# PEER's v sums of each layer's first pair of blocks as a dense product with a streamed table, and gathers in stages of u and of v

## The reference

```python
sv, si = lax.top_k(s, PEER_TOPK)                       # s: (tokens, 8, 2, 128)
cand = sv[:, :, 0, :, None] + sv[:, :, 1, None, :]
cv, ci = lax.top_k(cand.reshape(Tb, PEER_HEADS, PEER_TOPK * PEER_TOPK), PEER_TOPK)
...
eidx = i1 * N_KEYS + i2
g = jax.nn.softmax(cv, axis=-1)
u = u_tab[eidx]
v = v_tab[eidx]
a = jax.nn.gelu(jnp.einsum('thkd,td->thk', u, xb).astype(jnp.float32), approximate=False)
return jnp.einsum('thk,thkd->td', (g * a).astype(v.dtype), v)
```

## Time and profile before

| | |
|---|---|
| median of three runs | 3412.68 us (3407.83 to 3419.08) |
| the profiled execution | 3410.22 us, span 3408.4 us |
| TensorE busy | 2653.3 us (78%) |
| VectorE busy | 2352.5 us (69%) |
| GpSimd busy | 2260.1 us (66%) |
| ScalarE busy | 769.2 us (23%) |
| moved | 1187.53 MB, mean 348 GB/s |
| gathers | 1,024 of u and 1,024 of v |

### The profile page before, as it was taken

How to read it: one execution, slowest core, us unless ns; L and a number is a source line. 1 busy time by engine, 2 the same in 40 slices (tenths; PEclk the granted TensorE clock), 3 DMA queues, 4 the chain that set the end, 5 groups by cost and what they waited for, 6 DMA issues and landing times.

```text
span 3408.4 us, 30404 instructions
## 1 busy us (share of the span) xinstructions
PE 2653.3 (78%) x9120; PEld 1550.1 (45%) x9120; DVE 2352.5 (69%) x5335; ACT 769.2 (23%) x1848; POOL 2260.1 (66%) x2059
## 2 busy tenths in 40 slices
PE   8888079898987689778987679988987666556657
PEld 7677057556543256446543246656543222112212
DVE  2327975877689576877699666877689755666564
ACT  2531023442211123332111122442211111111111
POOL 0000276777777776777777776777677777777776
PEclk9879589989999999878999999989999989998899
DMA  5112399999999999999999999999999999999999
GB/s 184 59 50 92 115 385 412 366 322 392 410 362 358 388 410 412 390 331 381 410 381 379 358 383 411 378 322 367 410 394 355 364 401 409 409 409 408 410 409 349
DMA packets 311313, 1187.53 MB, mean 348 GB/s; under 512 B 34544, under 2 KB 34544, under 8 KB 298352
## 3 DMA queue, kind: packets, MB, share of 16 engines
q0 software_dynamic: 294912, 1073.87, 81.8%
q1 hardware_dynamic: 16240, 111.72, 8.4%
HBM read 1183.36 MB, written 2.10 MB: 348 GB/s over the span
## 4 chain that ended last, share of the span: by engine, by line
POOL 30%; PE 26%; DMA 22%; issue 10%; DVE 4%; ACT 1%; ACTq 0%; DVEq 0%; POOLq 0%
DMA v_rows<-expert_v,idx 22%; POOL u_rows L1455 16%; POOL v_rows L1468 15%; PE acc L741 14%; PE bank L457 4%; PE bank L448 4%; DVE arena L1030 1%; PE bank L620 1%; PE bank L439 1%; DVE arena L1288 0%; PE bank L540 0%; DVE arena L1280 0%; DVE arena L1292 0%; DVE X L1410 0%; DVE arena L1318 0%
## 5 line engine op out<-in xcount | busy, mean ns | idle before, releaser
L741 PE MATMUL acc<-v_rows,diag 128*128 128x512 f32 x2988 | 1533.6, 647 | 647.4 <-DMA v_rows<-expert_v,idx 575.6
L1393 DVE CUSTOM_DVE_ANT_0 u_rows<-u_rows,h 128x1024 f32<-128x1024 f32 x1024 | 1247.9, 1224 | 650.5 <-DMA u_rows<-expert_u,idx 646.1
L1455 POOL DMA_INDIRECT u_rows<-expert_u,idx x1024 | 1122.4, 1096 | 685.4 <-DVE idx L1357 348.9
L1468 POOL DMA_INDIRECT v_rows<-expert_v,idx x1024 | 1133.9, 1107 | 404.3 <-issue 249.3
L741 PEld LDWEIGHTS acc<-v_rows,diag 128*128 128x128 f32 x2988 | 560.1, 203 | 1453.1 <-issue 1177.3
L1021 ACT ACTIVATE diag<-consts,wgt 128x128 f32<-128x128 f32 x747 | 286.2, 397 | 1097.8 <-PE acc L741 882.2
L448 PE MATMUL bank<-HT,w_ring 128*128 128x256 f32 x1792 | 405.1, 381 | 2.1 <-DVE HT L1030 2.1
L1410 DVE SCALAR_TENSOR_TENSOR X<-v_rows,wgt,X 128x1024 f32<-128x1024 f32 x277 | 355.7, 1284 | 56.4 <-DMA v_rows<-expert_v,idx 50.7
L448 PEld LDWEIGHTS bank<-HT,w_ring 128*128 128x128 f32 x1792 | 341.3, 191 | 81.3 <-issue 38.7
L457 PE MATMUL bank<-w_ring,HT 128*128 128x256 f32 (+1 forms) x1280 | 274.7, 372 | 0.0
L457 PEld LDWEIGHTS bank<-w_ring,HT 128*128 128x128 f32 x1280 | 236.7, 191 | 50.0 <-issue 21.4
(11 more groups left out here) (185 smaller groups left out, 1860.1 us busy)
## 6 DMA issues: line engine op xcount, KB each, us to landing
w_ring<-weights SPq DMA_DIRECT2D x100, 1024.0 KB, 8.0
u_rows<-expert_u,idx POOLq DMA_INDIRECT x1024, 7.9
v_rows<-expert_v,idx POOLq DMA_INDIRECT x1024, 7.9
X<-in_x SPq DMA_DIRECT2D x2, 1024.0 KB, 6.5
out<-X SPq DMA_DIRECT2D x4, 512.0 KB, 6.5
n2w_wide<-parameters SPq DMA_DIRECT2D x2, 512.0 KB, 8.0
params<-parameters SPq DMA_DIRECT2D x2, 412.0 KB, 7.8
consts<-constants SPq DMA_DIRECT2D x1, 749.5 KB, 6.3
```

The lines of the kernel that those rows point to most:

```text
L741: last = T.matmul(acc[:, at_h], diag[:, i % DIAG_RING], v_rows[:, t % V_RING, at_h], start=(at_t == 0), stop=(t == max(q for q in range(t ...
L1393: made(V.tensor_tensor_reduce(out=rows_u, in0=rows_u, in1=h2[:], scale=1.0, scalar=0.0, op0=ALU.mult, op1=ALU.add, accum_out=dots[:, b % 2 ...
L1455: pool.indirect_dma_start(out=u_rows[:, s % U_RING, :], out_offset=None, in_=u_dram, in_offset=bass.IndirectOffsetOnAxis(ap=idx[:, (n - 1) ...
L1468: pool.indirect_dma_start(out=v_rows[:, t % V_RING, :], out_offset=None, in_=v_dram, in_offset=bass.IndirectOffsetOnAxis(ap=idx[:, t // PE ...
```

## The change

The gathers are now in stages of 256: the two blocks of one pair for u, or for v.

```diff
-PAIRS = BLOCKS // 2
-STEPS = DEPTH * PAIRS
-U_RING, V_RING, DIAG_RING = 6, 6, 5
-LAG = TOPK + 4
-TRUNK_AT, ROUTE_AT, DONE_AT = LAG + 2, 146, PER_STEP - 3
+GROUPS = [(0, 0, 2), (0, 2, 2), (1, 0, 2), (1, 2, 2)]
+STAGE = 2 * SLOTS
+STAGES = [("u", 0, 1), ("u", 1, None), ("v", 1, 2), ("u", 2, 3), ("u", 3, None), ("v", 3, None)]
+GATHERS = STAGE * len(STAGES)
+FOUR, GROUPS_OF_FOUR = 4, P // 4
+ROWS, DIAG_RING = 12, 5
+BESIDE_HOTS, BESIDE_STREAM, STREAM = 10, 6, 3
+EARLY = 40
+ALONE = 18
+def beside(n):
+    at = [e for e, (_, _, m) in enumerate(STAGES) if m == n][0]
+    lo, hi = STAGE * at + (2 if STAGES[at][0] == "u" else 8), STAGE * (at + 1) - 16
+    return lo, lo + (hi - lo) * 58 // 100, hi
+def of_vector(e, r):
+    n = STAGES[e][2]
+    if r < ALONE:
+        return True
+    if n is None:
+        return r % 4 == 3
+    return r % 8 != 0 if STAGE * e + r < beside(n)[1] else r % 3 == 0
```

```diff
+                        hot = hots[i % 2][:, 0]
+                        for t in range(FOUR):
+                            at_t = FOUR * i + t
+                            ins = S.activation(hot[:, t], iota, ACT.Abs, scale=-1.0, bias=first_keyT[:, at_t:at_t + 1])
+                        chain(ins)
+                        made(S.activation(hot, hot, ACT.Relu, scale=-1.0, bias=1.0), "hot1")
...
+                        bank = wait_full(act, f"d{d}.s{b}.{i - 1}")
+                        four = slice(FOUR * (i - 1), FOUR * i)
+                        freed(S.activation(gates[b][:, :, four].rearrange("p i t -> p t i"), bank[:].rearrange("p (t i) -> p t i", t=FOUR), ACT.Copy),
+                              f"d{d}.s{b}.{i - 1}")
...
+                        ins = V.tensor_scalar(hots[i % 2][:, 1, t], iota, second_keyT[b][:, at_t:at_t + 1], weightT[:, at_t:at_t + 1],
+                                              ALU.is_equal, ALU.mult)
...
+                        last = T.matmul(out[:, blk[t]], hots[i % 2][:, 0, t], hots[i % 2][:, 1, t], start=True, stop=True)
```

`gates` of both blocks take 128 KB of each partition, the place of the trunk's tiles (`arena`), the weight ring and `X` of the first pair, which is written to `out` and read back. Then SyncE streams the layer's v table, 64 transfers of two keys (1 MB), and TensorE adds up:

```diff
+                    sy.dma_start(rows[:, at_r:at_r + 2], table[d, :, 2 * j * D:2 * (j + 1) * D].rearrange("i (j d) -> i j d", j=2)
+                                 ).then_inc(sig(f"stream{j % STREAM}"), 16)
...
+                pe.wait_ge(sig(f"stream{j % STREAM}"), 16 * stream_use(d, j))
+                for i in range(2):
+                    key, row = 2 * j + i, rows[:, BESIDE_STREAM + 2 * (j % STREAM) + i]
+                    for b in (1, 0):
+                        for half in range(2):
+                            last = T.matmul(sums[b][half][:, 0:512], gates[b][:, key], row[:, 512 * half:512 * half + 512],
+                                            start=(key == 0), stop=(key == KEYS - 1))
...
+                made(last, "down")
```

Where this stands among the gathers is a second table of slots. Block 0's gates are made beside the end of the first u stage, block 1's at the start of the second, and the product fills the rest of it:

```diff
+    for b, lo, hi in ((0, first + 162, first + STAGE - 4), (1, first + STAGE + 2, first + STAGE + EARLY + 3)):
...
+    lo, hi = first + STAGE + EARLY + 4, first + 2 * STAGE + 4
+    out += [(f"d{j}", lo + (hi - lo) * j / (KEYS // 2)) for j in range(KEYS // 2)]
+    return out + [("xa", hi + 1)]
```

u and v rows now share one ring of 12 row slots. While gates are made u has ten of them, the one-hots two; beside the stream u has six and the stream six. A v gather into a slot that the stream used waits for it:

```diff
+                if kind == "v" and row >= BESIDE_STREAM and (had is None or had // STAGE < e):
+                    wait_down(pool, m // 2, KEYS // 2 - STREAM + (row - BESIDE_STREAM) // 2 + 1)
```

More of the change, by code:

```diff
@@ L181, in phases @@
     tail += [("g0", 0, .4), ("g1", 0, 0), ("g2", 0, 1.2)]
-    return head + middle + cmp_ + att + tail
-PHASES = phases()
-ORDER = {name: i for i, (name, *_) in enumerate(PHASES)}
-assert len(ORDER) == len(PHASES)
-def slots():
-    work = np.array([max(cost) + .5 for _, *cost in PHASES])
-    at, out = ORDER["r0"], []
-    for part, lo, hi in ((work[:at], TRUNK_AT, ROUTE_AT), (work[at:], ROUTE_AT, DONE_AT)):
+    every = head + middle + cmp_ + att + tail
+    if nb == 2:
+        return every
@@ new lines, in phases, with slots @@
+    of_block = ("n1t", "n1e", "xt", "xe", "xp", "dl", "cb", "de", "dm", "yp", "ya", "ys", "nt", "ne", "nc", "nd", "ng", "mt", "me", "n2t", "n2e")
+    return [(x, pe / 2, dve / 2) for x, pe, dve in every if not (x[:3] in of_block and x[3:4] == "1" or x[:2] in of_block and x[2:3] == "1")]
+PHASES = [phases(nb) for _, _, nb in GROUPS]
+ORDER = [{name: i for i, (name, *_) in enumerate(p)} for p in PHASES]
+assert all(len(o) == len(p) for o, p in zip(ORDER, PHASES))
+def slots(n):
+    work = np.array([max(cost) + .5 for _, *cost in PHASES[n]])
+    lo, route, hi = beside(n)
+    at, out = ORDER[n]["r0"], []
+    for part, lo, hi in ((work[:at], lo, route), (work[at:], route, hi)):
@@ L603, in keys @@
                     full(last, f"{n}.nt{b}")
[L604 to L605 removed]
+                out = take(pe, f"{n}.kc", f"ne{nb - 1}")
+                for b in range(nb):
                     last = T.transpose(out[:, blk[b]], nA[:, b, 0:128], ident)
@@ new lines, in tensor_program @@
+        def tensor_program(pe):
+            trunk_run(0, tensor_tracks(pe, 0)).all()
+            run = spread = None
+            for s in range(GATHERS):
+                n, d = starts(s)
+                if n is not None:
+                    run = trunk_run(n, tensor_tracks(pe, n))
+                if d is not None:
+                    spread = dense_run(d, [tensor_dense(pe, d)])
+                if KIND[s] == "v" and not BY_VECTOR[NTH_OF_KIND[s]]:
+                    t, b, at_t = v_slot(s)
+                    by_tensor = [q for q in range(SLOTS) if not BY_VECTOR[t - at_t + q]]
@@ new lines, in pool_program @@
+            trunk_run(0, pool_tracks(pool, 0, chain)).all()
+            run = None
+            for s in range(GATHERS):
+                n, _ = starts(s)
+                if n is not None:
+                    run = trunk_run(n, pool_tracks(pool, n, chain))
+                e, r = divmod(s, STAGE)
+                kind, m, beside_n = STAGES[e]
+                if r == 0 and kind == "u":
+                    pool.wait_ge(sig("idx"), m + 1)
+                row, use, had = ROW_OF[s]
+                if had is not None:
+                    wait_rows_used(pool, had)
+                if kind == "v" and row >= BESIDE_STREAM and (had is None or had // STAGE < e):
+                    wait_down(pool, m // 2, KEYS // 2 - STREAM + (row - BESIDE_STREAM) // 2 + 1)
+                pool.indirect_dma_start(
+                    out=rows[:, row, :], out_offset=None, in_=u_dram if kind == "u" else v_dram,
+                    in_offset=bass.IndirectOffsetOnAxis(ap=idx[:, m % 2, r:r + 1], axis=0),
+                ).then_inc(sig(f"row_in{row}"), 16)
+                if beside_n is not None:
+                    run.after(s - POOL_LAG)
+                    if r == STAGE - 1:
+                        run.all()
```

977 lines of the change are left out of this document (577 added, 400 removed).

## The result

The changed kernel takes 3571.04 us (median of four runs, 3564.33 to 3580.46), beside 3412.86 (3407.83 to 3419.08) for the kernel before on the same chip: 1.0465 times as long, with a 95% interval of 1.0435 to 1.0495. The forecast was 3,480 (2% slower), its range 3,345 to 3,620. The profiled execution took 3580.46 us, at a span of 3578.7.

A forecast was written before the change was run, and what follows sets the result against it. Transfers were taken to bound the kernel before; afterwards each stage has another engine as its bound. 397 + 578 + 543 + 500 + 570 + 543 + 345 + 4 = 3,480 us, 2% slower, range 3,345 to 3,620.

The forecast's parts named there:

- Stages 0: The first trunk alone, the same work as before: 397 us until `idx` is written.
- B: u gathers of a second pair beside the first pair's dense product: 543 us, twice; ScalarE bound first, then TensorE.
- C2: The last stage, v gathers of the second pair with no trunk beside it: 345 us (335 to 365).
- A1: First stage with u gathers of a first pair beside the second's trunk: 578 us, VectorE becoming the bound.
- A2: The same stage as A1 the second time, with no landing to wait for: 570 us.
- its 285: Part before routing in A1 and A2: VectorE 225 us, TensorE 218, and 60 of waits (15 to 110).
- 0.2 us for a one-hot of VectorE: In the routing part of A1 and A2, 32 groups of 4 one-hot instructions: 26 us (20 to 35).
- C1: v gathers of the second pair with a trunk beside them: 500 us, of which 281 before routing and 185 routing.
- Rival 1: Waits of the three trunk stages vanish, VectorE's dots filling the trunk's holes: up to 180 us less, 3,300; chance 0.27.
- Rival 2: ScalarE's strided write of the gates out of PSUM makes a group take 3.6 us: 3,575 us; chance 0.12.
- Rival 3: The stream transfers' wide pitch holds the queues twice as long, 175 us more in each B: 3,830; chance 0.04.

The follow-up runs named there:

- before_thin: The kernel before, with TensorE's v sums cut to 64 of 512 columns, all but a block's first and last: 3411.05 us.
- act_hot2: The changed kernel with block 0's second-key one-hots, weighted, made by ScalarE in place of VectorE: 3518.87 us, 1.0323 times the kernel before.
- split74: The changed kernel with 74 in place of 58 in 100 of a u stage's slots before routing: 3552.13 us, 1.0429 times the kernel before.

## Why the prediction was right in its direction and wrong in its size

- *Transfers bound the kernel before; the change saves 335 us of them, and the stages lose more.* Right in direction: 335 would have been the gain by its own sum, 158 is the loss.
- *Stages 0, B and C2.* Right to 7 us each. B: 94 us until the product starts (93 forecast), with ScalarE busy for 85 us of them, and 442 for the product (446), TensorE full at a clock of 1.00.
- *A1 and A2, 578 and 570 us: wrong, 621 and 614.* The step that failed is "TensorE about 620 - 332 = 288 less routing's 70, 218 us". It takes TensorE's time for the trunk from a step in which 332 us of dense v sums stood between its products, and removes the sums alone. Measured: 298 us. The kernel before has 238 us for the trunk up to its first key product, or 253 counted by the trunk's own records, so 20 to 35 of the 80 us were the subtraction. The other 45 to 60 are the clock, which the prediction put at nothing in this term: before_thin loses 65 us of TensorE's time for the same records. With 298 TensorE is the longer of the two and not VectorE, on whose 225 us (251 measured) the forecast built its 285. So the base is 298 - 225 = 73 us larger. The waits beside it are 343 - 298 = 45 us, and 60 + 8 of landing had been taken, 23 more: 73 - 23 = 50 us, which is what the part before routing took over its 293. "VectorE becomes the bound" was right behind the first key product (98 in 100 busy) and wrong before it (73 in 100); over the whole stage it is 84 in A1 and 85 in A2, which hides both.
- *0.2 us for a one-hot of VectorE, 26 us.* Four take 1.12 us in the trace, 0.28 each, 36 us; act_hot2, without them, has A stages shorter by 29 and 23 us, so most of them lies on the stage's path. The parts behind the first key product took 278 us, for 285 forecast, so these 10 us were made good by other terms of that part that were too large, which is luck.
- *C1, 500 us: 518.* In part the same failed step: 330 us before routing for 294. TensorE was busy for 265 us of them, at a clock of 0.84, where 246 were taken; the other 17 us are waits. Beside routing and behind it 188, for 185 and 21, so 18 of the 36 us were made good there.
- *Rival 1 (the waits vanish).* Its mark was waits in A under 20 us; VectorE is idle for 92 us of A1's part before routing. split74 shows that the holes can't be filled at will. Its price for C1 was too low besides: it gives TensorE 252 us for the trunk, where the forecast's own terms make 220 + 70 = 290.
- *Rival 2 (ScalarE's strided write).* The doubling is real, 591 to 1,046 ns; the two dependences it was to come with cost next to nothing, and the group takes 2.64 us, not 3.6. Right in part, and without weight. The Trainium skill ("SBUF — State Buffer", Door 1: The DMA port swizzle) has the penalty for each new 16-byte line that the prediction cited; that this write took 1,046 ns where the flat one took 579 agrees with it, though no run here varied the stride.
- *Rival 3 (the stream's pitch).* Refuted: a stream transfer lands after 8.0 us, a weight slot after 7.9, and TensorE's product into `bank` waited 3.2 us in all. The rate that the Trainium skill ("DMA: Bandwidth & Descriptors", Latency and other measured facts) gives for such a pitch was measured on copies of 16 KiB rows between HBM tensors. It was not seen in these loads of 8 KB rows into SBUF: the windows with the stream moved 407 and 398 GB/s.

The page's DMA issues of the changed kernel, KB and median us to landing, and the group of the product, in which rival 3 would have shown:

```profile
rows<-expert_v SPq DMA_DIRECT2D x128, 1024.0 KB, 8.0
arena<-weights SPq DMA_DIRECT2D x100, 1024.0 KB, 7.9
...
L913 PE MATMUL bank<-rows,arena 128*128 128x512 f32 x1024 | 484.9, 596 | 3.2 <-ACT arena L1236 2.8
```

Open: how much of an A stage the clock alone is worth (30 to 45 us is an estimate), and whether a kernel with the trunk's small products packed more densely would hold the upper clock.

## What to carry to other kernels

In these kernels the durations of small TensorE products held only for the neighbours they had: when a change takes dense work out from between them, price them at both clock levels, and put the longer one into the sum where the stage also stops being bound by transfers, since DMA no longer covers the loss. And price the new order of the stages apart from the saved bytes: here the staging alone cost some 390 us and the dense product gave 229 back.

## What the runs showed of the hardware that was not expected

- TensorE's granted clock was 0.50 and 0.59 in two windows of 60 us in which its records show it busy for 50 and 58 us: the page's busy digits don't tell of the clock, PEclk does. In before_thin cutting the v sums from 512 to 64 columns, at the same slots, took the clock around the score products from 0.95 to 0.50 and made them as slow as in the changed kernel.
- Raising it by added work lengthened the stage by less than that work: with 27 us added the A stages changed by +5 and -8 us, with 61 by +14 and +25, and in C1 70 us more of busy time cost 44. Only at the -8 did a stage become shorter, and A1 and A2 of the changed kernel differ by about as much (621 and 614).
- Four `tensor_scalar` of VectorE over 128 columns with two per-partition operands take 1.12 us, 0.28 each, against the 0.2 that the prediction took between the records of 154 ns (one column) and 354 ns (256 columns).
